# A hybrid decoder layer with mixture of experts: gathers, gain rows and scatter pieces in another order

## The chip, the core and the metric

One core of a Trainium2 chip runs the whole layer as one program. The metric is the device time in microseconds from the first to the last instruction of the core, as the median of three runs. All data are float32. TensorE's matmuls appear in the trace as two records each, one for each pass over a float32 operand, so that "x16" is eight matmuls.

## What is computed

The reference runs one decoder layer over two groups of tokens with shared weights: a prompt of 256 tokens and 8 samples of 8 new tokens each, with 256 cached keys and values behind every sample (D = 1024, 16 heads, 32 experts, 4 chosen for each token). Cut to what matters:

```python
def trunk_layer(x, c, lw, ...):
    ada = silu(c) @ w_ada + b_ada              # shift1, scale1, gate1, shift2, scale2, gate2
    h = rms_norm(x, g_mix_pre) * (1 + sc1) + sh1
    out, st = mixer(h, ...)                    # RG-LRU branch + forgetting attention, @ w_out
    x = x + gt1 * rms_norm(out, g_mix_post)
    h = rms_norm(x, g_ffn_pre) * (1 + sc2) + sh2
    f = moe(h, ...)
    return x + gt2 * rms_norm(f, g_ffn_post)

def expert_block(xb, e):
    gu = xb @ w_gate_up[e] + b_gate_up[e]
    x_glu = minimum(gu[:, :1024], 7.0)
    x_lin = clip(gu[:, 1024:], -7.0, 7.0)
    act = x_glu * sigmoid(1.702 * x_glu) * (x_lin + 1.0)
    return act @ w_down[e] + b_down[e]
```

moe picks the top 4 of 32 experts by softmax of the router's logits and adds up each token's four expert rows with their weights. The outputs are both groups' rows and the new keys, values, log forget values and states.

## The kernel before

Every engine has its own list of instructions, written out by hand and in order; engines meet only at semaphores (`s["name"]`, counted up by the one and waited for by the other). TensorE works in program order, so whatever it waits for holds up all that stands behind it. PSUM is eight banks B[0] to B[7] of 128 x 512 floats.

The stages in order of time: conditioning, input projections and the attention of the prompt (to about 345 us), then a loop over the 8 samples (b = 0 to 7) that carries the prompt's output projection, second norm, router and ranks in its gaps, then the samples' own output projection, norm and router (about 474 to 498 us), the first gather (to 511 us), the loop over 16 pairs of experts (to about 1455 us), and the final norm.

Weights stream through `ring`, twelve units of 1 MB, used as six slots of two units each. SyncE issues the transfers in order, one of 2048 KB for each slot; for each pair eight for gate and up (`gu_slot`, two for each two tiles, one for each expert of the pair) and four for down (`dn_slot`). Before each it waits until the counter `used` says that TensorE has read the slot's former contents: the ones for gate-up tiles 6 and 7 (counted from 0) wait for tile 1 of the same pair, those for down wait for tiles 3 and 5, the next pair's first two wait for tile 7, and the next four for the down tiles 3 and 7.

The loop of pairs treats 64 slots for each of two experts. On TensorE (`pair`, below) a pair is: eight gate-up tiles (k = 0 to 7, eight matmuls each, into B[0] to B[3]), with the former pair's results scattered to the tokens in between (`combine`, behind k = 0, 1, 2, through B[6] and B[7]), the transposes of the weighted selection behind k = 5 and the bias matmuls behind k = 6; then `gather`, which makes four of the eight column groups of inputs for a later pair (three matmuls for each, two over 128 prompt rows and one over 64 sample rows, B[4] and B[5]); then the transposes of the activation, which wait for VectorE (`act_made`); then eight down tiles into B[4] and B[5]. VectorE clips glu and lin once all eight gate-up tiles are done (`used` at 24), multiplies and adds; ScalarE does the sigmoids and copies PSUM to SBUF. Tile k = 0 needs the gathered inputs (`XT_made`). The loop is a hardware loop of four rounds with four pairs unrolled in each (u = 0 to 3).

The first gather makes the inputs of the first two pairs: eight column groups m, each with two prompt matmuls (K = 128) and one sample matmul (K = 64), in the halves of four banks. The prompt's part of the selection `sel` is ready early (`sel_made` 1), the samples' part (`sel_made` 2) only after their router, top 4 and ranks on VectorE. The post-norm gain rows (`G3`, comp = 5) are made by matmuls with an identity column (`gain_of_prompt`) or with rows of the sample table (`gain_of_sample`), and copied by ScalarE. They are used only in the final norm.

Line 1272 is the transposes' helper and line 1736 the matmuls of `both`, which serves gate-up, bias and down tiles. `hT` and `work` in a row tell which buffer holds the gathered inputs (activations are in `work`).

Of the kernel before, what the change touches and what calls it, by code (L numbers as in the profile page):

```python
# [31 lines left out]
def hybrid_layer(nc, x_prompt, x_sample, cache_k, cache_v, cache_logf, state_conv, state_h, page_table,  # L32
# [11 lines left out]
    NT = D // 128  # L44
    SP_, DB, DS = x_prompt.shape[1], x_sample.shape[0], x_sample.shape[1]
    NS = DB * DS
# [14 lines left out]
    NPC = 5  # L61
    EPS, LIMIT, ALPHA, SCALE, LRU_C = 1e-6, 7.0, 1.702, float(HD) ** -0.5, 8.0
# [5 lines left out]
    with ctx:  # L68
# [131 lines left out]
        def piece(v, i):  # L200
            return v[:, 512 * i:512 * i + 512]

        x1 = kf
        G3 = gaf[:, 0:1536]
# [239 lines left out]
        def _(eng):  # L444
# [73 lines left out]
            eng.wait_ge(s["router_ps"], 2)  # L518
# [28 lines left out]
        def _(eng):  # L547
# [107 lines left out]
            for b in range(DB):  # L655
                if b + 2 < DB:
                    keys(b + 2)
                if b + 1 < DB:
                    probs(b + 1)
                if b + 2 < DB:  # L660
                    sexps(b + 2)
                if b == 0:
                    for n, i in enumerate((0, 2, 1, 3)):
                        if n % 2 == 0:
                            eng.wait_ge(s["gain_ps"], n // 2 + 1)
                            A_(piece(G1, n // 2), B[7][:, :], ACT.Copy).then_inc(s["G1_made"], 1)
                        eng.wait_ge(s["op_ps"], n + 1)
                        A_(piece(tokf, i), B[5 + n % 2][:, :], ACT.Square, accum_out=ss[:, i:i + 1]).then_inc(s["op_sq"], 1)
                    root(r1, 2)
                if b == 1:  # L670
                    for i in range(4):
                        eng.wait_ge(s["x1_made"], i + 1)
                        A_(piece(tokf, i), piece(x1, i), ACT.Square, accum_out=ss[:, 4 + i:5 + i]).then_inc(s["x1_sq"], 1)
                    root(r2, 3)
                if b == 3:
                    for k in range(2):
                        for h in range(2):
                            eng.wait_ge(s["h2T_ps"], 2 * k + h + 1)
                            A_(h2P[:, 4 * h:4 * h + 4, 128 * k:128 * k + 128], B[5 + h][:, :].rearrange("p (m n) -> p m n", m=4),
                               ACT.Copy).then_inc(s["h2T_made"], 1)  # L680
                if b == 4:
                    eng.wait_ge(s["topmax_made"], 1)
                    A_(tope[:, 0:2, 0:TOPK], tope[:, 0:2, 0:TOPK], ACT.Exp).then_inc(s["topexp_made"], 1)

# [12 lines left out]
            eng.wait_ge(s["op_ps"], 5)  # L697
            for i in range(3):
                eng.wait_ge(s["G3_ps"], i + 1)
                A_(piece(G3, i), B[3 + i][:, :], ACT.Copy).then_inc(s["G3_made"], 1)  # L700

# [8 lines left out]
            XT_out(0, 0, 1, 0)  # L710
            for i in range(2):
                eng.wait_ge(s["gather_ps"], 3 + i)
                A_(XT[0][:, 4 + 2 * i:6 + 2 * i, :], B[6 - 4 * i][:, :].rearrange("p (t s) -> p t s", t=2), ACT.Copy)\
                    .then_inc(s["XT_made"], 1)

            def pair(t, i, u):
                eng.wait_ge(s["cT_ps"], t + 1)
# [5 lines left out]
                XT_out(1 - u // 2, u % 2, 2 * t + 5, 4)  # L723
# [9 lines left out]

            for i in range(NPC):
                eng.wait_ge(s["scatter_read"], NPC * done + i + 1)
                A_(piece(work[:, 2048:4608], i), piece(gbf, i), ACT.Square, accum_out=ss[:, 10 + i:11 + i]).then_inc(s["f_sq"], 1)
# [3 lines left out]
        def _(eng):  # L740
# [450 lines left out]
            V_.tensor_copy(C[0:E, :], B[4][0:E, 0:T]).then_inc(s["C_made"], 1)  # L1191
# [55 lines left out]
            def combined(t, n):  # L1247
                eng.wait_ge(s["scatter_ps"], NPC * t + n + 1)
                TTo(piece(gbf, n), piece(gbf, n), B[6 + n % 2][:, :], ALU.add).then_inc(s["scatter_read"], 1)  # L1249
# [5 lines left out]
            for n in range(NPC):  # L1255
                eng.wait_ge(s["f_sq"], n + 1)
                link.later(TTo(piece(gbf, n), piece(gbf, n), piece(G3, n if n == 1 else (0, 1, 0, 1, 2)[n]), ALU.mult))
# [10 lines left out]
        def _(eng):  # L1268
# [333 lines left out]
            for b in range(DB):  # L1602
# [24 lines left out]
                if b == 5:  # L1627
                    ranks_of_prompt()
                sfold(b)
            eng.wait_ge(s["wt_made"], 6)  # L1630
# [20 lines left out]
            def gather_first(m, tiles):  # L1651
                out = B[GBANK[m // 2]][:, QUAD * (m % 2):QUAD * (m % 2) + QUAD]
                for k in tiles:
                    q = 64 * (m // 4)
                    if k < 2:
                        last = mm(out, tok[:, k, 128 * m:128 * m + 128], sel[:, k, :], start=(k == 0), stop=False)
                    else:
                        last = mm(out, tok[q:q + 64, 2, 128 * (m % 4):128 * (m % 4) + 128], sel[q:q + 64, 2, :], start=False, stop=True)
                return last
# [4 lines left out]
            for m in (0, 2):  # L1664
                gather_first(m, (0, 1))
            eng.wait_ge(s["x1_sq"], 5)
            both_halves(1)
            eng.wait_ge(s["mo_made"], 5)
            for m in (4, 6):
                gather_first(m, (0, 1))  # L1670
# [3 lines left out]
            last.then_inc(s["h2T_ps"], 1)  # L1674
            eng.wait_ge(s["h2T_made"], 5)
# [7 lines left out]
            for h in range(2):  # L1683
                gain_of_prompt(B[3 + h], 5, h).then_inc(s["G3_ps"], 1)
            gain_of_sample(B[5], 5).then_inc(s["G3_ps"], 1)
# [3 lines left out]
            mm(B[7][:, 224:256], ones[0:64, :], chosen[0:64, 2, :], start=True, stop=True).then_inc(s["rank_ps"], 1)  # L1689
            eng.wait_ge(s["sel_made"], 2)  # L1690
            for m in range(NT):
                last = gather_first(m, (0, 1, 2) if m % 2 else (2,))
                if m % 2:
                    last.then_inc(s["gather_ps"], 1)
# [12 lines left out]
            eng.wait_ge(s["G3_made"], 2)  # L1707
            for k in range(TT):
                last = tr(B[4][0:E, 128 * k:128 * k + TROWS[k]], wtok[0:TROWS[k], k, :], TROWS[k])
# [5 lines left out]
            def combine(t, pieces):  # L1715
                for n in pieces:
# [5 lines left out]
                    k, bank = n // 2, B[6 + n % 2]  # L1722
                    if k < 2:
                        last = mm(bank[:, :], C[:, 128 * k:128 * k + 128], Ysb[:, 512 * (n % 2):512 * (n % 2) + 512], start=True, stop=True)  # L1724
                    else:
                        for h in range(2):
                            last = mm(bank[64 * h:64 * h + 64, :], C[:, SP_:T], Ysb[:, 512 * h:512 * h + 512], start=True, stop=True)
# [11 lines left out]
            def pair(t, i, u):  # L1739
                slots = XT[u // 2][:, :, SL * (u % 2):SL * (u % 2) + SL]  # L1740
                ready = 2 * t + (2 if u % 2 == 0 else 0)
                for k in range(NT):
# [9 lines left out]
                    if k < 3:  # L1752
                        combine(t, ((0, 1), (2, 3), (4,))[k])
                    if k == 5:
# [7 lines left out]
                    if k == 6:  # L1762
# [3 lines left out]
                if u % 2 == 0:  # L1766
                    eng.wait_ge(s["sel_made"], t + 4)
                gather(u % 2, 4)
# [18 lines left out]
            eng.wait_ge(s["f_sq"], NPC)  # L1787
# [34 lines left out]
```

## Time and profile before

| what | value |
|---|---|
| runs, median (lowest to highest) | 1473.31 us (1472.67 to 1474.71) |
| profiled execution, span | 1472.5 us |
| TensorE busy | 1379.4 us, 94% of the span |
| VectorE, ScalarE, GpSimd busy | 340.9, 231.5, 25.5 us |
| mean granted TensorE clock | 0.966 |
| HBM read | 481.63 MB, 330 GB/s over the span |
| chain that ended last | TensorE 76%, DMA 17%, issue 2%, VectorE 2%, ScalarE 2% |
| gate-up transfers in that chain | 16% |

Times are from the start of the span. The profiled execution is one run of its own; its span stands 0.8 us below the median of the timed runs. "Busy" of TensorE counts matmuls whose ends are modelled. A clock of 1.00 is 2.4 GHz and the lower level is 1.2 GHz; a mean between them is a share of time at either. In a timeline row the bracket tells how long the engine was idle before it and what released it.

### The profile page before, as it was taken

What the parts mean: (1) busy time and instruction counts of PE and PEld (TensorE: products, weight loads), DVE (VectorE), ACT (ScalarE), POOL (GpSimd) and SP (SyncE); (2) the same over time, 40 slices, a digit from 0 to 9 for tenths busy, and PEclk for the clock granted to TensorE, in tenths of its full rate; (3) what the DMA queues carried; (4) which work ended last, traced back from release to release, by engine and by line L of the source; (5) the groups of instructions that cost most, each with busy time, mean ns of one, the idle gap of its engine ahead of it and who ended that gap; (6) DMA issues with size and microseconds to landing.
All of it is one profiled execution on the core that took longest, in us unless ns stands there. A gap on an engine that the chain in (4) does not pass through costs nothing.

```text
span 1472.5 us, 15902 instructions
## 1 busy us (share of the span) xinstructions
PE 1379.4 (94%) x6323; PEld 627.4 (43%) x6323; DVE 340.9 (23%) x715; ACT 231.5 (16%) x459; POOL 25.5 (2%) x56
## 2 busy tenths in 40 slices
PE   5999799999988999999999999999999999999996
PEld 3555356666445433434334334333343333433432
DVE  2541412444143320102201111021021010120113
ACT  2113301433251200101111001011010011110102
POOL 1100000001000000000000000000000000000000
PEclk9999899999986899999999999999999999999998
DMA  9836355543056589999999999999999999999992
GB/s 329 258 127 252 111 211 187 189 147 122 15 173 239 214 337 419 428 428 426 429 426 427 428 421 427 430 426 427 426 425 429 426 414 414 422 429 428 428 427 104
DMA packets 72477, 486.84 MB, mean 331 GB/s; under 512 B 10349, under 2 KB 15205, under 8 KB 47828
## 3 DMA queue, kind: packets, MB, share of 16 engines
q1 hardware_dynamic: 70724, 480.85, 80.0%
q0 software_dynamic: 1680, 4.91, 1.0%
q8 instruction: 58, 0.95, 0.3%
q14 instruction: 15, 0.12, 0.0%
HBM read 481.63 MB, written 4.12 MB: 330 GB/s over the span
## 4 chain that ended last, share of the span: by engine, by line
PE 76%; DMA 17%; issue 2%; DVE 2%; ACT 2%; SPq 1%; DVEq 0%; ACTq 0%; PEldq 0%
PE bank L1736 35%; DMA ring<-in_w_gate_up_dram 16%; PE bank L1383 9%; PE bank L1701 5%; PE bank L1410 4%; PE bank L1272 4%; PE bank L1724 3%; PE bank L1702 3%; PE bank L1364 2%; PE bank L1570 2%; PE bank L1527 1%; DMA ring<-in_w_ada_dram 1%; PE bank L1376 1%; PE bank L1363 1%; PE bank L1638 1%
## 5 line engine op out<-in xcount | busy, mean ns | idle before, releaser
L1736 PE MATMUL bank<-ring,work 128*64 128x512 f32 x2048 | 457.6, 600 | 17.7 <-issue 10.3
L1736 PEld LDWEIGHTS bank<-ring,work 128*64 128x64 f32 x2048 | 161.4, 138 | 292.1 <-issue 291.8
L1736 PE MATMUL bank<-ring,hT 128*64 128x512 f32 x1024 | 233.9, 603 | 14.8 <-DMA ring<-in_w_gate_up_dram 14.8
L1249 DVE TENSOR_TENSOR gbT<-gbT,bank 128x512 f32<-128x512 f32 x85 | 58.5, 688 | 452.5 <-PE bank L1724 391.9
L1383 PE MATMUL bank<-hT,ring 128*128 128x320 f32 x512 | 143.4, 440 | 2.4 <-DVE hT L767 1.7
L1736 PEld LDWEIGHTS bank<-ring,hT 128*64 128x64 f32 x1024 | 77.2, 138 | 160.1 <-issue 160.1
L1383 PEld LDWEIGHTS bank<-hT,ring 128*128 128x128 f32 x512 | 97.7, 193 | 50.4 <-issue 8.6
L1218 DVE TENSOR_SCALAR work<-bank 128x512 f32<-128x512 f32 x32 | 22.0, 687 | 323.2 <-PE bank L1736 323.2
L1410 PE MATMUL bank<-hT,ring 128*128 128x320 f32 x256 | 72.4, 436 | 0.0
L1701 PE MATMUL bank<-qT,tok 128*128 128x256 f32 x256 | 72.4, 405 | 0.0
L718 ACT ACTIVATE work<-bank 128x320 f32<-128x320 f32 x16 | 7.0, 437 | 409.9 <-PE bank L1272 409.9
L1724 PE MATMUL bank<-work 128*128 128x512 f32 x136 | 67.4, 618 | 1.2 <-ACT work L730 1.2
L1701 PEld LDWEIGHTS bank<-qT,tok 128*128 128x128 f32 x256 | 43.4, 189 | 32.2 <-issue 28.9
L1410 PEld LDWEIGHTS bank<-hT,ring 128*128 128x128 f32 x256 | 47.4, 190 | 20.1 <-issue 2.3
L730 ACT ACTIVATE work<-bank 128x512 f32<-128x512 f32 x32 | 17.4, 595 | 217.6 <-PE bank L1736 217.6
L1272 PE MATMUL bank<-ident,work 128*128 128x128 f32 (+4 forms) x253 | 44.6, 296 | 6.0 <-DMA work<-in_b_ada_dram 4.0
L1364 PE MATMUL bank<-ring 128*32 128x512 f32 x192 | 29.9, 716 | 19.8 <-DMA ring<-in_w_ada_dram 10.8
L721 ACT ACTIVATE work<-work 128x512 f32<-128x512 f32 x32 | 20.1, 630 | 166.9 <-DVE work L1218 166.9
L1702 PE MATMUL bank<-qT,tok 64*128 64x256 f32 x128 | 44.5, 428 | 0.0
L1272 PEld LDWEIGHTS bank<-ident,work 128*128 128x128 f32 (+4 forms) x253 | 30.5, 175 | 32.6 <-issue 30.1
L1724 PEld LDWEIGHTS bank<-work 128*128 128x128 f32 x136 | 22.9, 189 | 45.1 <-issue 41.8
L1272 PE MATMUL bank<-ident,ring 128*128 128x128 f32 (+2 forms) x139 | 23.9, 329 | 8.1 <-ACT work L637 7.2
(336 smaller groups left out, 882.5 us busy)
## 6 DMA issues: line engine op xcount, KB each, us to landing
ring<-in_w_gate_up_dram SPq DMA_DIRECT2D x128, 2048.0 KB, 14.8
ring<-in_w_down_dram SPq DMA_DIRECT2D x64, 2048.0 KB, 17.0
ring<-in_w_ada_dram SPq DMA_DIRECT2D x12, 2048.0 KB, 9.9
ring<-in_w_in_dram SPq DMA_DIRECT2D x12, 2048.0 KB, 9.9
ring<-in_cache_k_dram SPq DMA_DIRECT2D x16, 512.0 KB, 5.9
ring<-in_cache_v_dram SPq DMA_DIRECT2D x16, 512.0 KB, 4.5
ring<-in_w_out_dram SPq DMA_DIRECT2D x2, 2048.0 KB, 7.7
out_dram<-tok POOLq DMA_DIRECT2D x2, 1024.0 KB, 5.2
```

The lines of the kernel that those rows point to most:

```text
L721: A_(sig[:, 512 * j:512 * j + 512], glu[:, 512 * j:512 * j + 512], ACT.Sigmoid, scale=ALPHA)\
L1218: TS(glu[:, half[j]], B[j][:, :], LIMIT, None, ALU.min).then_inc(s["glu_made"], 1)
L1249: TTo(piece(gbf, n), piece(gbf, n), B[6 + n % 2][:, :], ALU.add).then_inc(s["scatter_read"], 1)
L1272: return nc.tensor.transpose(out, in_, ident[0:rows, 0:rows])
L1364: last = mm(ps[32 * g:32 * g + 32, :], silu_c[:, k, :], w[0][:, k, :], start=(k < 4), stop=(k >= 4))
L1383: last = mm(ps[:, 0:T], w[0][:, k, 128 * (t % 4):128 * (t % 4) + 128], hT[:, k, :], start=(k == 0), stop=(k == NT - 1))
L1410: last = mm(B[4 + h % 2][:, 0:T], w[0][:, k, 128 * (h % 4):128 * (h % 4) + 128], hT[:, k, :], start=(k == 0), stop=(k == NT - 1))
L1570: last = mm(B[5 + t][:, :], gaT[:, k, 128 * t:128 * t + 128], w[h][:, k, :], start=(k == 0), stop=(k == NT - 1))
L1701: mm(out, tok[:, k, 128 * m:128 * m + 128], sel[:, k, :], start=(k == 0), stop=False)
L1702: last = mm(out, tok[q:q + 64, 2, 128 * (m % 4):128 * (m % 4) + 128], sel[q:q + 64, 2, :], start=False, stop=True)
L1724: last = mm(bank[:, :], C[:, 128 * k:128 * k + 128], Ysb[:, 512 * (n % 2):512 * (n % 2) + 512], start=True, stop=True)
L1736: last = mm(bank[CAP * x:CAP * x + CAP, :], lhsT[:, CAP * x:CAP * x + CAP], rhs(x), start=start, stop=stop)
```

## The change

Five edits, in the order of the program.

1. Gain rows of the final norm: they are made in the samples' loop, one each at b = 5, 6, 7, instead of behind the samples' router, and go into the prompt columns of gaT (`G3(i)`, a view of two blocks of 256). ScalarE copies each at the end of its step.
2. First gather: all prompt matmuls of all eight m's stand ahead of the samples' selection, spread over the waits of the samples' norm and router. The two m's of a bank form one accumulation group. The sample matmuls follow in the order 0, 4, 1, 5, 2, 6, 3, 7, so that rows 0 to 63 and 64 to 127 take turns. The transposes of the routing weights go to B[7] instead of B[4], so C is copied in two pieces. The gate-up bias rows' DMAs no longer wait for the samples' router.
3. In a pair, `gather` runs behind the fifth gate-up tile (k = 4) instead of behind the eighth, and the bias matmuls behind k = 5 instead of k = 6. ScalarE copies the gathered rows first in the pair.
4. Scatter pieces run in the order 4, 0, 1, 2, 3 (the sample's first).
5. In the tail, a Sqrt of one element on ScalarE stands ahead of the squares, and the sum of the samples' halves waits for the first square instead of all five.

```diff
+    SCATTER = (4, 0, 1, 2, 3)
-        G3 = gaf[:, 0:1536]
+        def G3(i):
+            return gaT[:, 2 * i:2 * i + 2, 0:SP_]
@@ gpsimd
-            eng.wait_ge(s["router_ps"], 2)
             for j in range(4):
                 eng.dma_start(bgu[E * j:E * j + E, :], ...)
@@ scalar
+                if b >= 5:
+                    eng.wait_ge(s["G3_ps"], b - 4)
+                    A_(G3(b - 5), B[5 + b % 2][:, :].rearrange("p (t n) -> p t n", t=2), ACT.Copy).then_inc(s["G3_made"], 1)
...
-            eng.wait_ge(s["op_ps"], 5)
-            for i in range(3):
-                eng.wait_ge(s["G3_ps"], i + 1)
-                A_(piece(G3, i), B[3 + i][:, :], ACT.Copy).then_inc(s["G3_made"], 1)
...
-            XT_out(0, 0, 1, 0)
-            for i in range(2):
-                eng.wait_ge(s["gather_ps"], 3 + i)
-                A_(XT[0][:, 4 + 2 * i:6 + 2 * i, :], B[6 - 4 * i][:, :].rearrange("p (t s) -> p t s", t=2), ACT.Copy)\
-                    .then_inc(s["XT_made"], 1)
+            for i, (m, bank) in enumerate(((0, 0), (4, 6), (2, 1), (6, 2))):
+                eng.wait_ge(s["gather_ps"], 1 + i)
+                A_(XT[0][:, m:m + 2, :], B[bank][:, :].rearrange("p (t s) -> p t s", t=2), ACT.Copy).then_inc(s["XT_made"], 1)
             def pair(t, i, u):
+                XT_out(1 - u // 2, u % 2, 2 * t + 5, 4)
                 eng.wait_ge(s["cT_ps"], t + 1)
...
-                XT_out(1 - u // 2, u % 2, 2 * t + 5, 4)
                 for j in range(2):
                     eng.wait_ge(s["aT_ps"], 2 * t + (j + 1))
...
-            for i in range(NPC):
-                eng.wait_ge(s["scatter_read"], NPC * done + i + 1)
+            A_(sst[:, 0, 0:1], ones[:, 0:1], ACT.Sqrt)
+            for n, i in enumerate(SCATTER):
+                eng.wait_ge(s["scatter_read"], NPC * done + n + 1)
@@ vector
-            V_.tensor_copy(C[0:E, :], B[4][0:E, 0:T]).then_inc(s["C_made"], 1)
+            link.later(V_.tensor_copy(C[0:E, 0:SP_], B[7][0:E, SP_:2 * SP_]))
+            link(V_.tensor_copy(C[0:E, SP_:T], B[7][0:E, 0:NS]))
+            eng.sem_inc(s["C_made"], 1)
@@ tensor, samples' loop
                 if b == 5:
                     ranks_of_prompt()
+                    gain_of_prompt(B[6], 5, 0).then_inc(s["G3_ps"], 1)
+                if b == 6:
+                    gain_of_prompt(B[5], 5, 1).then_inc(s["G3_ps"], 1)
+                if b == 7:
+                    eng.wait_ge(s["wt_made"], 6)
+                    eng.wait_ge(s["G3_made"], 1)
+                    gain_of_sample(B[6], 5).then_inc(s["G3_ps"], 1)
                 sfold(b)
-            eng.wait_ge(s["wt_made"], 6)
+            eng.wait_ge(s["G3_made"], 3)
             gain_of_sample(B[6], 2).then_inc(s["gains_ps"], 1)
@@ tensor, first gather
+            def gather_prompt(m):
+                for k in range(2):
+                    mm(first_out(m), tok[:, k, 128 * m:128 * m + 128], sel[:, k, :], start=(m % 2 == 0 and k == 0), stop=False)
+            def gather_sample(m):
+                q = 64 * (m // 4)
+                return mm(first_out(m), tok[q:q + 64, 2, 128 * (m % 4):128 * (m % 4) + 128], sel[q:q + 64, 2, :],
+                          start=False, stop=(m % 2 == 1))
             eng.wait_ge(s["sel_made"], 1)
-            for m in (0, 2):
-                gather_first(m, (0, 1))
+            gather_prompt(0)
+            gather_prompt(1)
...
+            eng.wait_ge(s["mo_made"], 5)
+            gather_prompt(4)
             eng.wait_ge(s["h2T_made"], 5)
...
-            for h in range(2):
-                gain_of_prompt(B[3 + h], 5, h).then_inc(s["G3_ps"], 1)
-            gain_of_sample(B[5], 5).then_inc(s["G3_ps"], 1)
+            gather_prompt(5)
+            gather_prompt(6)
             eng.wait_ge(s["chosen_made"], 2)
...
+            gather_prompt(7)
             eng.wait_ge(s["sel_made"], 2)
-            for m in range(NT):
-                last = gather_first(m, (0, 1, 2) if m % 2 else (2,))
-                if m % 2:
-                    last.then_inc(s["gather_ps"], 1)
+            for m in range(4):
+                for q in (m, m + 4):
+                    last = gather_sample(q)
+                    if m % 2:
+                        last.then_inc(s["gather_ps"], 1)
@@ tensor, pair
+                    if k == 4:
+                        if u % 2 == 0:
+                            eng.wait_ge(s["sel_made"], t + 4)
+                        gather(u % 2, 4)
                     if k == 5:
...
-                    if k == 6:
                         eng.wait_ge(s["esel_made"], t + 1)
                         for j in range(4):
                             both(B[j], esel[E * j:E * j + E, :], lambda x: bgu[E * j:E * j + E, :], False, False)
-                if u % 2 == 0:
-                    eng.wait_ge(s["sel_made"], t + 4)
-                gather(u % 2, 4)
                 for j in range(2):
                     eng.wait_ge(s["act_made"], 2 * t + (j + 1))
...
-            eng.wait_ge(s["f_sq"], NPC)
+            eng.wait_ge(s["f_sq"], 1)
```

## Rows read from the trace of the kernel before

**Rows 1.** The page: the span, and the DMA engines' busy tenths in forty slices.
```profile
span 1472.5 us, 15902 instructions
...
DMA  9836355543056589999999999999999999999992
```

**Rows 2.** Stages by pair: busy us and count of PE, PEld, DVE, ACT, POOL; clock, DMA share, GB/s.
```profile
611.00:672.00 61.00, 58.29 (x258) 22.72 (x258) 9.66 (x16) 5.38 (x11) 0.00 (x0) 0.97 1.01 429
672.00:729.00 57.00, 56.24 (x255) 21.70 (x255) 9.43 (x15) 4.89 (x10) 0.00 (x0) 1.00 1.00 427
```

**Rows 3.** The chain in order of time, where a pair's down tiles begin.
```profile
554.56 17.39 PE bank L1736 x80
...
611.26 17.39 PE bank L1736 x80
...
1440.97 13.97 PE bank L1736 x64
```

**Rows 4.** TensorE's waits from 511 to 1456 us: total, times, longest.
```profile
PE bank L1736 <- DMA ring<-in_w_gate_up_dram: 21.5, 13, 2.1
```

**Rows 5.** The chain inside one pair: the transfer that the seventh gate-up tile waits for.
```profile
1108.08 18.67 DMA ring<-in_w_gate_up_dram
```

**Rows 6.** Timeline of the same pair, from the end of the eighth gate-up tile on.
```profile
1135.10 1.13 PE L1701 MATMUL bank<-qT,tok 128*128 128x256 f32 x4
...
1138.22 0.68 DVE L1231 TENSOR_TENSOR work<-work 128x512 f32<-128x512 f32 x1
...
1139.54 0.69 DVE L1231 TENSOR_TENSOR work<-work 128x512 f32<-128x512 f32 x1
...
1141.85 1.23 PE L1272 MATMUL bank<-ident,work 128*128 128x128 f32 x8
...
1143.32 3.22 PE L1736 MATMUL bank<-ring,work 128*64 128x512 f32 x14 [0.25 <-issue]
```

**Rows 7.** Timelines of TensorE around idle gaps, in the samples' loop and the pairs.
```profile
410.97 1.10 PE L1272 MATMUL bank<-ident,ring 128*128 128x128 f32 x8 [0.23 <-DMA ring<-in_cache_k_dram]
416.30 1.97 PE L1272 MATMUL bank<-ident,ring 128*128 128x128 f32 x8 [4.24 <-ACT work L637]
...
949.16 3.65 PE L1736 MATMUL bank<-ring,hT 128*64 128x512 f32 x16 [2.12 <-DMA ring<-in_w_gate_up_dram]
981.51 5.35 PE L1736 MATMUL bank<-ring,work 128*64 128x512 f32 x16 [1.96 <-issue]
```

**Rows 8.** Timeline of the first gather, from the gain rows to the first gate-up tile.
```profile
494.01 1.13 PE L1550 MATMUL bank<-xT,ident 32*128 32x512 f32 x4
...
497.43 0.42 DVE L1122 TENSOR_TENSOR qT<-xT,qT 128x256 f32<-128x256 f32 x1
...
499.06 2.07 PE L1656 MATMUL bank<-qT,tok 128*128 128x256 f32 x4
...
509.18 1.13 PE L1656 MATMUL bank<-qT,tok 128*128 128x256 f32 x4
510.24 0.70 PE L1658 MATMUL bank<-qT,tok 64*128 64x256 f32 x2
...
511.81 3.65 PE L1736 MATMUL bank<-ring,work 128*64 128x512 f32 x16 [0.39 <-ACT work L713]
```

**Rows 9.** Timeline of the samples' loop: one gain row alone, then steps six and seven.
```profile
371.15 1.12 PE L1550 MATMUL bank<-xT,ident 32*128 32x512 f32 x2
...
464.38 1.93 PE L1527 MATMUL bank<-ring,work 128*32 128x256 f32 x16 [3.13 <-DVE gbT L1018]
...
467.95 0.99 PE L1534 MATMUL bank<-work 128*128 128x32 f32 x4
...
472.83 1.06 PE L1534 MATMUL bank<-work 128*128 128x32 f32 x4 [0.55 <-DVE work L1010]
```

**Rows 10.** Timeline of the tail.
```profile
1461.65 3.09 DVE L1257 TENSOR_TENSOR gbT<-gbT,gaT 128x512 f32<-128x512 f32 x5
...
1462.51 1.28 ACT L553 ACT_TABLE_LOAD   x1
```

More of the change, by code:

```diff
@@ L1248, in combined @@
                 eng.wait_ge(s["scatter_ps"], NPC * t + n + 1)
-                TTo(piece(gbf, n), piece(gbf, n), B[6 + n % 2][:, :], ALU.add).then_inc(s["scatter_read"], 1)
+                i = SCATTER[n]
+                TTo(piece(gbf, i), piece(gbf, i), B[6 + n % 2][:, :], ALU.add).then_inc(s["scatter_read"], 1)
             done = moe_rounds(eng, pair)
@@ L1254, in _ @@
             eng.wait_ge(s["G3_made"], 3)
-            for n in range(NPC):
+            for n, i in enumerate(SCATTER):
                 eng.wait_ge(s["f_sq"], n + 1)
-                link.later(TTo(piece(gbf, n), piece(gbf, n), piece(G3, n if n == 1 else (0, 1, 0, 1, 2)[n]), ALU.mult))
+                v = piece(gbf, i).rearrange("p (t n) -> p t n", t=2)
+                link.later(TTo(v, v, G3(2 if i == 4 else i % 2), ALU.mult))
             halves(r3[:, 0:2], ss[:, 10:14])
@@ L1649, in _, with first_out @@
             GBANK = (0, 1, 6, 2)
[L1651 to L1659, printed above, removed]
+            def first_out(m):
+                return B[GBANK[m // 2]][:, QUAD * (m % 2):QUAD * (m % 2) + QUAD]
+            def gather_prompt(m):
[5 more added lines that the diff above has]
+                          start=False, stop=(m % 2 == 1))
             eng.wait_ge(s["op_sq"], 5)
@@ L1663, in _ @@
             eng.wait_ge(s["sel_made"], 1)
-            for m in (0, 2):
-                gather_first(m, (0, 1))
+            gather_prompt(0)
+            gather_prompt(1)
             eng.wait_ge(s["x1_sq"], 5)
             both_halves(1)
-            eng.wait_ge(s["mo_made"], 5)
-            for m in (4, 6):
-                gather_first(m, (0, 1))
+            gather_prompt(2)
+            gather_prompt(3)
             eng.wait_ge(s["h2tok_made"], 5)
@@ L1706, in _ @@
             eng.wait_ge(s["wtok_made"], 2)
-            eng.wait_ge(s["G3_made"], 2)
             for k in range(TT):
-                last = tr(B[4][0:E, 128 * k:128 * k + TROWS[k]], wtok[0:TROWS[k], k, :], TROWS[k])
+                o = SP_ + 128 * k if k < 2 else 0
+                last = tr(B[7][0:E, o:o + TROWS[k]], wtok[0:TROWS[k], k, :], TROWS[k])
             last.then_inc(s["wt_ps"], 1)
@@ L1721, in combine @@
                         eng.wait_ge(s["scatter_read"], NPC * t + (n - 1))
-                    k, bank = n // 2, B[6 + n % 2]
+                    i, bank = SCATTER[n], B[6 + n % 2]
+                    k = i // 2
                     if k < 2:
-                        last = mm(bank[:, :], C[:, 128 * k:128 * k + 128], Ysb[:, 512 * (n % 2):512 * (n % 2) + 512], start=True, stop=True)
+                        last = mm(bank[:, :], C[:, 128 * k:128 * k + 128], Ysb[:, 512 * (i % 2):512 * (i % 2) + 512], start=True, stop=True)
                     else:
```

## The prediction

> **What bounds the kernel now.** I read the page's slices first: over the loop of pairs TensorE is busy nearly all the time (94% of the whole span) and, from slice 14 on, the DMA engines are at nine tenths or more [rows 1]. Two things are that full at once, so the question is which of them ends last, and by how much. The stages by pair of experts answer it [rows 2]: DMA share 1.00 and some 427 GB/s in every pair, TensorE busy 58.29 of 61 us in one and 56.24 of 57 in the next. A pair brings twelve transfers of 2048 KB (2.097 MB); at 427 GB/s one takes 4.91 us and twelve take 58.9. The first down tile of pair 0 starts at 554.56 and that of pair 15 at 1440.97 [rows 3]: 886.4 us for 15 periods, 59.1 each. So the mean pair is the DMA's. How far behind is TensorE? The pair from 554.56 to 611.26 has no wait for a transfer: 56.7 us. That is TensorE's own need, and the whole slack is 59.1 - 56.7 = 2.4 us. The waits confirm it: 21.5 us for gate-up weights in 13 waits, over 16 pairs [rows 4]. In the chain a pair therefore alternates between TensorE and the wait for the seventh gate-up tile's weights [rows 5].
>
> **The move of a pair's gathers.** Before, the eight gathers stand between the eighth gate-up tile and the activation's transposes. The timeline of a pair [rows 6] shows what they do there. TensorE ends that tile at 1135.10. VectorE and ScalarE then need the clips, sigmoids and products: the first half of the activation is ready at 1138.22 + 0.68 = 1138.90, the second at 1139.54 + 0.69 = 1140.23. The gathers run from 1135.10 to 1141.85, 6.7 us, and hide all of it; transposes and 0.25 of issue bring the down tiles to 1143.32, 8.2 us after the tile's end. After the change the gathers run behind the fifth gate-up tile and still take 6.7. But nothing is left to cover the activation. Transposes of half 0 can start 3.8 us after the eighth tile; those of half 1 wait until 5.1, take 0.6 (half of 1.23), and with 0.25 of issue the down tiles start 6.1 us after the tile's end. ScalarE's copies of half 0 are done by then, because the gathered rows' copies have moved out of its way. So a pair costs TensorE 6.7 + 6.1 - 8.2 = 4.6 us more: about 61.3 instead of 56.7. That is more than the DMA's 58.9, and the bound changes hands.
>
> Does the DMA queue keep up? SyncE issues two slots' transfers whenever their counter is passed. The transfers for tiles seven and eight are issued after the second tile and wanted at the seventh, some 25 us later with the gathers now in between. They took 18.7 us with a full queue [rows 5]; with over 2 us of slack in each period the queue drains, so less. The next pair's first two are issued after the eighth tile, which comes about 4.6 us later within the pair, and are wanted only after a whole down stage of 13.8 us plus 6.1. TensorE waits for none of them. What goes in return: the 21.5 us of waits, and what they cost in clock. The fetch stalls of some 2 us at the loop's branch (three in all, one stands at 981.51 [rows 7]) stay.
>
> **The clock.** After idle gaps of about 2.1 us the granted clock sometimes fell to the lower level, 1.2 GHz: the tile behind the gap took 5.35 us instead of 3.65, 1.70 more, at 981.51, but not at 949.16 [rows 7]. Five of the loop's sixteen stages show 0.97 for this reason (one of them in rows 2); three of the falls stood behind DMA waits (3 x 1.7 = 5.1 us, returned with them). The new gap is 3.8 us, then 0.6 of transposes, then 0.7 of idle. No gap of the loop is that long. The nearest outside it is 4.24 us before 416.30: eight transposes then took 1.97 instead of 1.10 [rows 7], 0.9 more, with the low clock reaching on into the work behind them. So I expect a fall in most pairs, costing 0.9 to 1.7 us each; I take 1.5, nearer the rows inside the loop. Bounds: 0 (as at 949.16) and 2.5 (a longer low stretch, as from 499 to 506, where groups of gathers took 2.07 instead of 1.13 [rows 8]). The Trainium skill (TensorE: Matmul & The Clock Gate, section HAM oscillation) says that idle phases between bursts let the clock fall again and again, each time at a price. By that rule the fall comes in all 16 pairs, and the sum below stands as it is.
>
> **First gather.** Before, select of the sample ends at 497.43 + 0.42 = 497.85 and the first pair starts at 511.81, 14.0 us: gathers until 510.87, part at the low clock, then ScalarE's last copy, which releases the first tile [rows 8]. After, all sixteen prompt matmuls have run ahead: four of the m's as before, one in the wait for the copy of h2T, two in place of the post-norm rows from 494.01 on, one while VectorE ranks. Behind select stand eight sample matmuls, 0.53 each at 256 columns and the high clock (four records of line 1656 in 1.06, as at 509.18). Do two row halves overlap? Two post-norm rows from different row quarters (the four records at 494.01) took 1.13 together, as one alone does (two records at 371.15, 1.12; the next group starts 1.05 later in both cases) [rows 8, 9]; so four steps of 0.53, 2.1 us, then two of ScalarE's copies, about 0.6 each, and hand-over, about 4.0 in all. The Trainium skill (TensorEngine Tiling, section Key Properties) says that row tiles load and multiply in parallel and that a change of tiling mode drains the array. By it the halves take 2.1 us too. Without overlap they take 8 x 0.63 = 5.0 (0.63 is what two records of line 1658 advance). Gain 14.0 - 4.0 = 10.0; 0.4 is lost because one m's prompt gathers (1.05) are longer than the wait of about 0.7 that they fill.
>
> **Post-norm rows in the samples' loop.** One such row costs 1.05 at the high clock, so about 2.0 at the low one. The first is hidden: TensorE idles 3.13 us before 464.38. The second sits between the transposes and the fold at 467.95, for which VectorE and then the next values wait: 1.05 to 2.0, all on the path. The third stands before the fold at 472.83, behind 0.55 of idle: 0.5 to 1.45 [rows 9]. Sum 1.6 to 3.5; the stretch is mostly at the low clock, so I take 2.5. ScalarE's copies (0.60) hide behind the fold (0.99). Net start of the loop: 10.0 - 0.4 - 2.5 = 7.1 us earlier; bounds 3 (no overlap, low clock) and 9.
>
> **The rest, at nothing.** The tail's early Sqrt saves a table load of 1.28 at 1462.51 that ends at 1463.79, while VectorE multiplies until 1464.74 [rows 10]: hidden already; uncovered it would be worth 1.3. The order of pieces and the earlier sum move at most 0.1. The gate-up bias rows come earlier on GpSimd's queue; nothing of the loop's start waits for them before, where ScalarE's last copy released it [rows 8]. The two chained copies of C (one small instruction more, some 0.3) end before the first combine; if they did not, that 0.3 would count once.
>
> **Sum against the profiled 1472.5.** 16 x (4.6 + 1.5) = +97.6; waits and their clock back -(21.5 + 5.1) = -26.6; start -7.1. Together +63.9: 1536.4, and with the 0.8 by which the median of the runs (1473.3) stands above the profiled span, 1537.
>
> **Rivals.** (A) The clock holds in every gap: 16 x 4.6 - 26.6 - 7.1 = +40, 1513. For it: 949.16; against: that gap is half as long as the new one. (B) Other side, faster: the loop stays with the DMA, because the uncovered activation wait fits the slack, so that only the start's 7.1 is left, 1466. It decides by one number: it holds if the added TensorE time is under 2.2 us (58.9 - 56.7), and the rows give 4.6. (C) The low clock lasts some 7 us each time, 3.4 per pair: 16 x 8.0 - 33.7 = +94, 1568. For it: the stretch from 499 to 506; against: every fall inside the loop cost 1.7. (D) The halves don't overlap, so that part of the change doesn't do what it says: +2.9 on the forecast, 1540, inside the range.
>
> **How the numbers follow.** Forecast with D 0.68, A 0.15, C 0.08, B 0.07, 0.02 for a wash of gains and losses. Range: from no clock loss with the largest start gain, +73.6 - 26.6 - 9 = +38 (1511), to 2.5 per pair with the smallest, +113.6 - 26.6 - 3 = +84 (1557); rounded outward for the 0.2 us by which a reading per pair can be off, 1508 to 1560. It leaves out B and C. A measurement of this kernel can tell about 0.2%, 3 us, from no change. Faster 0.07, same 0.02, slower 0.91.
>
> **What would show it.** Periods between first down tiles of 61 to 64 us, all alike but for the branch; DMA share about 0.94 and some 400 GB/s; no wait for gate-up weights; a TensorE gap of 3.8 us behind each eighth tile ended by VectorE; first down tiles slowed, PEclk 0.96 to 0.97 in each pair; first pair near 504.7. I am wrong if the periods stay at 59, if the gap is below 2.2 us, or if TensorE still waits for weights.

## The result, and the profile after

The changed kernel takes 1537.3 us in the median (1533.8 to 1547.3), the kernel before 1473.2: 1.044 times as long, with a 95% interval of 1.041 to 1.048. The forecast was 1537.

The profiled execution of the changed kernel is its slowest, 1545.3 us. Three lines of its page, beside [rows 1]: the DMA engines are no longer full in every slice of the loop, and the chain has given up the transfers (1% instead of 17%) for TensorE and VectorE.

```profile
span 1545.3 us, 15904 instructions
...
DMA  8636365433247689999999999998999999999991
...
PE 88%; DVE 5%; issue 3%; ACT 2%; DMA 1%; SPq 0%; DVEq 0%; ACTq 0%; PEldq 0%
```

The same stages as in [rows 2], one pair each; the columns are the stretch, its length, the busy time of PE, PEld, DVE, ACT and POOL, the granted clock, DMA share and GB/s. Both clock and DMA share are now below 1.00 in every pair.

```profile
1068.90:1132.10 63.20, 58.99 (x258) 20.86 (x259) 9.49 (x15) 5.17 (x9) 0.00 (x0) 0.96 0.96 399
1132.10:1196.10 64.00, 59.64 (x257) 21.02 (x259) 9.44 (x16) 5.17 (x9) 0.00 (x0) 0.95 0.94 394
```

TensorE's waits inside the loop, which answer [rows 4]. The wait for gate-up weights is gone. In its place stand 32 waits for line 1233, VectorE's last product of each activation half, 66.4 us in all, or 4.15 a pair. Line 1276 is the transposes' helper here, and line 1752 the matmuls of `both`.

```profile
PE bank L1276 <- DVE work L1233: 66.4, 32, 3.8
PE bank L1752 <- issue: 6.3, 3, 2.2
```

The timeline of one pair from the end of its eighth gate-up tile on, which answers [rows 6]. The profile models that end at 1125.84; the prediction counted from the start of the next instruction, which overlaps it by 0.06, so that 1125.78 is the point to compare with 1135.10.

```profile
1125.89 0.69 DVE L1220 TENSOR_SCALAR work<-bank 128x512 f32<-128x512 f32 x1 [25.30 <-PE bank L1752]
...
1129.63 0.90 PE L1276 MATMUL bank<-ident,work 128*128 128x128 f32 x4 [3.79 <-DVE work L1233]
...
1130.95 1.13 PE L1276 MATMUL bank<-ident,work 128*128 128x128 f32 x4 [0.43 <-DVE work L1233]
...
1132.01 16.35 PE L1752 MATMUL bank<-ring,work 128*64 128x512 f32 x64
```

TensorE stands still for 3.79 us, transposes half 0, waits 0.43 for half 1 and starts the down tiles 6.2 us behind the eighth tile. The transposes take 0.90 and 1.13 instead of the 0.6 that is half of 1.23 in [rows 6], the down tiles 16.35 instead of 13.97 [rows 3]. The granted clock (before the DMA share) shows why:

```profile
1125.90:1130.00 4.10, 0.37 (x3) 0.38 (x4) 4.10 (x7) 1.26 (x2) 0.00 (x0) 1.00 0.99 424
1130.10:1136.80 6.70, 6.27 (x19) 2.29 (x19) 2.73 (x5) 1.20 (x2) 0.00 (x0) 0.50 1.00 428
```

It has fallen to the lower level behind the gap and stays there into the down tiles.

The first gather, beside [rows 8] and [rows 9]. First the gain rows at b = 6 and b = 7, then the select, the eight sample matmuls and the first gate-up tile.

```profile
475.79 2.07 PE L1554 MATMUL bank<-xT,ident 32*128 32x512 f32 x2
...
482.13 1.97 PE L1559 MATMUL bank<-xT 32*64 32x512 f32 x4
...
508.55 0.42 DVE L1122 TENSOR_TENSOR qT<-xT,qT 128x256 f32<-128x256 f32 x1
...
509.03 2.00 PE L1671 MATMUL bank<-qT,tok 64*128 64x256 f32 x16
...
512.50 3.65 PE L1752 MATMUL bank<-ring,work 128*64 128x512 f32 x16 [0.77 <-ACT work L713]
```

The whole difference between the two profiled spans, 72.8 us (1545.3 - 1472.5), by stretches:

| stretch | before | after | difference |
|---|---|---|---|
| start to a fixed point in the samples' loop (values, b = 4) | 440.27 | 447.98 | +7.7 |
| from there to the first gate-up tile | 71.5 | 64.5 | -7.0 |
| pair 0, to its first down tile | 42.8 | 47.9 | +5.1 |
| 15 periods between first down tiles | 886.4 (59.1 each) | 951.6 (63.4 each) | +65.2 |
| from the last pair's down tiles to the end | 31.5 | 33.4 | +1.8 |

The first row is no effect of the change. It arises before any changed instruction, by 40 us, and begins with the 48 records that turn x. The lines below are the changed kernel's, then the kernel before's:

```profile
19.14 14.18 PE L1297 MATMUL bank<-gbT,tok 128*128 128x128 f32 x48 [0.17 <-PE bank L1368]
...
19.05 8.45 PE L1293 MATMUL bank<-gbT,tok 128*128 128x128 f32 x48 [0.17 <-PE bank L1364]
```

The cause is when TensorE's clock first rises. The trace of the changed kernel has its first record of a granted clock, a rise to the full level, at 37.8 us; that of the kernel before has it at 19.8. The stretches of the profile count the time ahead of the first record as full, but the matmuls show that it was the lower level. In the changed kernel one form of matmul, 512 columns at line 1368, takes (its columns: shortest, median and longest in ns):

```profile
L1368 PE MATMUL bank<-ring x12: 1061/1061/1062, 35.1 to 36.8; 128*32 128x512 f32 x12
...
L1368 PE MATMUL bank<-ring x36: 592/592/657, 37.7 to 43.9; 128*32 128x512 f32 x36
...
L1368 PE MATMUL bank<-ring x32: 1033/1061/1062, 179.4 to 190.0; 128*32 128x512 f32 x32
```

The third line lies in a stretch that the profile itself gives as 0.50 (178 to 194 us). The profiled runs fall into two groups. In three (changed, e2, e5) the first rise stands at 37.6 to 38.1 us, and they are 7.4 to 8.1 us behind the kernel before at 40 us; in the other nine it stands at 17.7 to 19.8, and they are at most 1.2 us away from it. Why the rise comes late in some executions of the same work stays open.

A second chance of the same kind lies in the samples' loop. e1 and e10 below are one kernel (run on two chips; e1's own twelve runs lie between 1457.5 and 1472.4), yet their first gate-up tiles start at 498.46 and 504.61. The difference grows from 350 us on, where the low stretches that begin before 455 us add up to 13.7 us in e1 and 27.3 in e10. The two profiles of the result don't differ there: the changed one is 7.7 to 7.9 us behind all the way from 40 to 440 us. So the total of a single run carries a chance of 7 to 8 us at the start and of about 6 us in the samples' loop, and I read the loop of pairs by its periods and the start by intervals between fixed points.

### The profile page after: what moved, and what is told of

Its sections match the earlier page's. It is cut to its first block, busy times and chain, and to the rows that moved or that the text cites. A ratio compares the mean times of both kernels' runs of the same rounds, so it can differ in the third digit from the quotient of the medians.

```text
span 1545.3 us, 15904 instructions
## 1 busy us (share of the span) xinstructions
PE 1414.6 (92%) x6323; PEld 612.3 (40%) x6323; DVE 340.0 (22%) x716; ACT 233.4 (15%) x460; POOL 25.5 (2%) x56
## 4 chain that ended last, share of the span: by engine, by line
PE 88%; DVE 5%; issue 3%; ACT 2%; DMA 1%; SPq 0%; DVEq 0%; ACTq 0%; PEldq 0%
PE bank L1752 46%; PE bank L1387 9%; PE bank L1716 4%; PE bank L1740 4%; PE bank L1414 4%; PE bank L1276 4%; PE bank L1717 3%; PE bank L1574 2%; PE bank L1368 2%; DVE work L1228 1%; PE bank L1531 1%; PE bank L1743 1%; PE bank L1297 1%; DVE work L1233 1%; DMA ring<-in_w_ada_dram 1%
## 5 line engine op out<-in xcount | busy, mean ns | idle before, releaser
L1752 PE MATMUL bank<-ring,work 128*64 128x512 f32 x2048 | 475.3, 619 | 7.0 <-issue 6.3
L1752 PEld LDWEIGHTS bank<-ring,work 128*64 128x64 f32 x2048 | 146.7, 143 | 318.2 <-issue 318.2
L1752 PE MATMUL bank<-ring,hT 128*64 128x512 f32 x1024 | 229.9, 596 | 0.0
L1752 PEld LDWEIGHTS bank<-ring,hT 128*64 128x64 f32 x1024 | 69.7, 137 | 150.9 <-issue 150.9
L1276 PE MATMUL bank<-ident,work 128*128 128x128 f32 (+4 forms) x253 | 58.9, 355 | 72.4 <-DVE work L1233 66.4
L1276 PEld LDWEIGHTS bank<-ident,work 128*128 128x128 f32 (+4 forms) x253 | 36.0, 180 | 113.1 <-DVE work L1233 85.6
L1740 PE MATMUL bank<-work 128*128 128x512 f32 x136 | 71.6, 631 | 0.0
L729 ACT ACTIVATE work<-bank 128x512 f32<-128x512 f32 x32 | 17.4, 595 | 235.4 <-PE bank L1752 235.4
L708 ACT ACTIVATE hT<-bank 128x512 f32<-128x512 f32 x16 | 9.6, 597 | 223.8 <-PE bank L1717 223.8
L708 ACT ACTIVATE work<-bank 128x512 f32<-128x512 f32 x16 | 9.6, 598 | 220.4 <-PE bank L1717 220.4
L1740 PEld LDWEIGHTS bank<-work 128*128 128x128 f32 x136 | 21.5, 188 | 49.3 <-issue 47.4
```

The lines of the kernel that those rows point to most:

```text
L1276: return nc.tensor.transpose(out, in_, ident[0:rows, 0:rows])
L1752: last = mm(bank[CAP * x:CAP * x + CAP, :], lhsT[:, CAP * x:CAP * x + CAP], rhs(x), start=start, stop=stop)
```

## The experiments

From each trace I take the start of the first gate-up tile, the mean period (first down tile of pair 0 to that of pair 15, over 15) and what lies between that first tile and the end, which the chances ahead of it don't touch. The totals are medians of the timed runs, the ratios are against the kernel before on the same chip.

| kernel | total, us | ratio (95%) | mean period | first tile to end |
|---|---|---|---|---|
| before | 1473.2 | | 59.1 | 960.7 |
| changed | 1537.3 | 1.044 (1.041 to 1.048) | 63.4 | 1032.8 |
| e1 gathers back | 1462.8 | 0.993 (0.991 to 0.996) | 59.0 | 958.7 |
| e2 move alone | 1549.7 | 1.051 (1.045 to 1.056) | 63.4 | 1032.1 |
| e3 two late | 1467.1 | 0.997 (0.993 to 1.000) | 58.9 | 959.6 |
| e4 one late | 1504.4 | 1.022 (1.017 to 1.026) | 61.7 | 1005.0 |
| e5 filled gap | 1513.4 | 1.027 (1.023 to 1.030) | 61.9 | 1008.0 |
| e6 before, half down | 1447.6 | 0.983 (0.980 to 0.987) | 57.4 | 935.8 |
| e7 changed, half down | 1539.0 | 1.045 (1.041 to 1.049) | 63.6 | 1035.5 |

**e1: the move undone.** All other edits stay. ScalarE's copies of the gathered rows go back behind the sigmoids with it.

```diff
-                    if k == 4:
-                        ...
-                        gather(u % 2, 4)
...
+                gather(u % 2, 4)
                 for j in range(2):
                     eng.wait_ge(s["act_made"], 2 * t + (j + 1))
```

> The changed kernel with one thing undone: a pair's gathers stand behind the eighth gate-up tile again (and ScalarE's copies of them behind the sigmoids); all other edits stay. Theory (the move uncovered the activation wait and made TensorE the bound): the whole loss is gone and only the start's gain of 7 us is left, 1466 us, periods of 59.1 us, DMA share 1.00 in each pair. Rival (the loss comes from the other edits in or before the loop, or from the order of the pieces): it stays well above 1473.

Measured 1462.8, 0.66% (0.36 to 0.95%) below the kernel before, with periods of 59.0 and the DMA share back at 1.00. So the loss hangs on the move. The 10.3 us below the kernel before are more than the start's 7: from the first tile to the end the profile of e1 takes 2.0 us less than before, and the medians carry the chances named above. The waits for weights are back too, as more and on average shorter ones (13 waits in 21.5 us before [rows 4]):

```profile
PE bank L1752 <- DMA ring<-in_w_gate_up_dram: 22.4, 29, 2.4
```

**e2: the move alone**, in the kernel before: the same lines of `pair` moved on TensorE and on ScalarE, nothing at the start or in the tail.

> The kernel before with the move alone: gathers behind the fifth gate-up tile, the bias matmuls behind the sixth, ScalarE's copies first. Theory: 16 uncovered waits, +72 us as the profile of the changed kernel shows them (5.2 in pair 0, 65.2 over 15 periods, 1.7 behind the last), so 1545 us. Rival (the edits act together): not the sum of the two parts, below 1530 or above 1555.

From the first tile to the end it takes 71.4 us more than before, against 72.1 in the changed kernel. The total of 1549.7 is 77 above before; its four runs scatter from 1538 to 1555, and the profiled one carries the 14.18 at the start. Up to that scatter the parts add up: e2 is 76.6 and e1 -10.3 us from the kernel before, together 66.3, and the changed kernel 64.1. Nothing shows the edits acting on each other.

**e3 and e4: how much cover is enough.** Two column groups (e3) or one (e4) of four stay behind the eighth tile. In both, ScalarE copies the first two groups' rows first in the pair and the other two behind the sigmoids; these lines are left out here.

```diff
-                        gather(u % 2, 4)
+                        gather(u % 2, 4, range(0, 2))      # e4: range(0, 3)
...
+                gather(u % 2, 4, range(2, 4))              # e4: range(3, 4)
                 for j in range(2):
                     eng.wait_ge(s["act_made"], 2 * t + (j + 1))
```

> The changed kernel with the gathers split: two column groups behind the fifth tile, two (3.4 us) behind the eighth. Theory: the down tiles still start 6.1 us after the eighth tile, so TensorE needs 56.7 + 3.4 + 6.1 - 8.2 = 58.0 us a pair, under the transfers' 58.9: nothing is lost, 1466 to 1469 us. Rival (moving gathers ahead of the sixth to eighth tiles frees the ring's slots later and starves the DMA queue, in proportion to what is moved): half of the loss, about 1500 us.

> As the former, but three column groups behind the fifth tile and one (1.7 us) behind the eighth. Theory: TensorE needs 56.7 + 5.0 + 6.1 - 8.2 = 59.6 us a pair, just over the transfers' 58.9, and has a gap of 2.1 us in each, behind which the clock falls about every second time (0.8): with the branch's stalls some 60.5 to 60.9, so 1490 to 1498 us; 1478 if the clock holds. Rival (loss in proportion to what is moved): three quarters of it, 1520 us.

e3 has the loop of e1 (959.6 against 958.7 us) though half of the gathers moved. Its TensorE has gaps of 0.42 and 0.58 us in each pair, which the transfers' slack pays. The clock falls behind them in one pair of 16 (at 1188.4). A pair without wait or branch takes 57.8 us:

```profile
1012.00:1069.80 57.80, 56.80 (x257) 20.36 (x257) 9.18 (x14) 5.17 (x9) 0.00 (x0) 1.00 1.01 428
...
1067.77 0.75 PE L1277 MATMUL bank<-ident,work 128*128 128x128 f32 x4 [0.42 <-DVE work L1234]
1069.09 0.74 PE L1277 MATMUL bank<-ident,work 128*128 128x128 f32 x4 [0.58 <-DVE work L1234]
```

So the loss is not in proportion to what is moved, and earlier gathers don't starve the DMA queue. It begins between e3 and e4, where TensorE's need (57.8 us in e3, 59.6 by the working for e4) passes the transfers' 58.9. e4 is past that point, as expected, but with 61.7 rather than 60.5 to 60.9. The gap has the size I worked out, and what I mis-sized is how often the clock falls behind it:

```profile
1036.40 1.12 PE L1277 MATMUL bank<-ident,work 128*128 128x128 f32 x4 [2.10 <-DVE work L1234]
1037.72 1.13 PE L1277 MATMUL bank<-ident,work 128*128 128x128 f32 x4 [0.20 <-DVE work L1234]
```

A gap of 2.0 to 2.3 us in the loop before was followed by a fall in 5 of 11 cases [rows 7]. In e4 the trace has a fall in each of the 16 pairs. Here a second gap of 0.2 to 0.6 follows after one short burst; that this second gap makes the difference is likely but not tested. In the thirteen pairs whose down tiles the branch doesn't interrupt, they take 0.5 to 2.0 us longer than in e5, where the clock holds.

**e5: the gap filled.** Seven matmuls more in each pair, into a bank that nobody reads at that point.

```diff
+                for _ in range(7):
+                    mm(B[6][:, 0:256], tok[:, 0, 0:128], tok[:, 1, 0:256], start=True, stop=True)
                 for j in range(2):
                     eng.wait_ge(s["act_made"], 2 * t + (j + 1))
```

> The changed kernel with seven matmuls more in each pair, behind the eighth gate-up tile, into a bank that nobody reads (seven times 0.53 us = 3.7): they fill the wait for the activation and move nothing else. Theory (part of the loss is the clock, which falls in the gap): the clock stays at 1.00, the periods fall from 63.4 to 61.4 us and the time to about 1510 us. Rival (the wait alone is the loss, the clock costs nothing): 1537 us as before, or more if the fillers delay the transposes.

TensorE does more work and the kernel is 24 us faster than the changed one. Of the gaps only 0.57 and 0.58 us are left. The clock holds at 1.00 but for two falls behind the branch's stall (16 falls in the changed kernel), and a pair without the branch takes 61.2 us:

```profile
1056.70:1117.90 61.20, 60.05 (x272) 22.94 (x271) 9.19 (x14) 5.17 (x9) 0.00 (x0) 1.00 0.98 410
...
862.92 3.29 PE L1786 MATMUL bank<-tok 128*128 128x256 f32 x14
866.78 0.75 PE L1276 MATMUL bank<-ident,work 128*128 128x128 f32 x4 [0.57 <-DVE work L1233]
868.10 0.74 PE L1276 MATMUL bank<-ident,work 128*128 128x128 f32 x4 [0.58 <-DVE work L1233]
868.78 3.65 PE L1752 MATMUL bank<-ring,work 128*64 128x512 f32 x16
```

The mean period falls from 63.4 to 61.9: the clock costs 1.5 us a pair, the uncovered wait the other 2.8 above the 59.1 before.

**e6 and e7: fewer bytes.** Half of each down transfer is left out in both kernels, so half of each down slot holds older data and the expert outputs are not the layer's.

```diff
-                    eng.dma_start(dn_slot[g], dnv[g // 2, :, ds(2 * i + g % 2, 1), :, :]...)
+                    eng.dma_start(dn_slot[g][:, 0:2, :], dnv[g // 2, :, ds(2 * i + g % 2, 1), 0:2, :]...)
```

> The kernel before with half of each down transfer left out (the other half of the slot keeps older data), so that a pair brings ten transfers' worth of bytes instead of twelve: 49 us. Theory (the transfers bound it by 2.4 us a pair): waits for weights vanish, periods of 57.0 us, 1473 - 27 = 1446 us. Rival (TensorE bounds it already): 1473 us.

> The changed kernel with the same half of each down transfer left out. Theory (TensorE bounds it): no change, 1537 us within its scatter of some 5 us, periods of 63.4. Rival (the transfers still bound it, because the slots come free later): 20 us or more are gained.

Before: 25 us faster; a pair takes 56.9 us with the DMA engines 0.89 busy. Changed: nothing (1539.0 against 1537.3; 1.045 and 1.044 of the kernel before), with the DMA engines 0.82 busy. Each of the two was run twice.

```profile
1012.50:1069.40 56.90, 56.30 (x255) 21.81 (x256) 9.53 (x15) 5.09 (x10) 0.00 (x0) 1.00 0.89 369
```

```profile
933.50:995.70 62.20, 58.21 (x258) 20.86 (x259) 9.49 (x15) 5.17 (x9) 0.00 (x0) 0.97 0.82 338
```

This shows the exchange of bounds by itself: the transfers bound the kernel before and do not bound the changed one.

**e8: row halves in turn.** The kernel of e1 with the sample matmuls in the order 0 to 7.

> The kernel of e1 with the eight sample matmuls of the first gather in the order 0 to 7, so that rows 0 to 63 and 64 to 127 no longer take turns. Theory (two row halves run at once): 8 x 0.53 to 0.63 instead of 2.0 us for the eight, the loop starts 2.3 to 3 us later than in e1, 1469 us. Rival (the order makes no difference): 1466 us, as e1.

Measured 1462.8, as e1; the totals can't tell 3 us. The trace can. The eight matmuls in e8:

```profile
494.09 2.96 PE L1671 MATMUL bank<-qT,tok 64*128 64x256 f32 x16
```

2.96 us against 2.00 in e1, so the alternation saves 1.0 us and not 3. But the order 0 to 7 does not keep the halves apart, as I had meant it to. Line 1671 in three stretches, with the busy time and count of records of PE and PEld; the first two are e8's, the third e1's:

```profile
494.09:495.05 0.96, 0.96 (x4) 0.85 (x5) 1.00 0.87 358
495.06:495.80 0.74, 0.74 (x8) 0.73 (x7) 1.00 0.11 44
...
494.99:495.95 0.96, 0.96 (x8) 0.88 (x10) 1.00 0.68 273
```

In e8 one half works alone for 0.97 us, a record every 0.216; then the other half starts beside it and the records come twice as fast. In e1 both halves start together. The signals say the same: in e8 the records that report m = 3, 5 and 7 done start 1.62, 1.73 and 2.59 us behind the first record, so m = 5 of the second half ends just behind m = 3 of the first. In either order the four matmuls of one half take 1.99 us from first start to last end. One after the other the two halves would take 4.0 us by this, an estimate; in the changed order they take 2.00, and in e8 2.96 because half of the overlap is left. So the halves overlap fully, and e8 shows half of what that is worth.

On the way from select to the first tile only 0.4 of the 1.0 is left (3.91 us against 3.53). ScalarE's first copy starts 1.2 us behind the first sample matmul in both, and in e8 only the second one waits once more, 0.27 us. The prediction's size for no overlap was wrong as well: it took 0.63 for a K = 64 matmul from a sequence that mixes K = 64 and K = 128; within one half they take 0.43.

**e9: gain rows in the tail.** The kernel of e1 with the three rows out of the samples' loop, made behind the pairs; e10 is e1 beside it.

```diff
+            for h in range(2):
+                gain_of_prompt(B[h], 5, h).then_inc(s["G3_ps"], 1)
             combine(done, range(NPC))
+            gain_of_sample(B[2], 5).then_inc(s["G3_ps"], 1)
```

> The kernel of e1 with the three post-norm rows taken out of the samples' loop altogether: they are made behind the loop of pairs, the prompt's two in the 1.2 us in which TensorE waits for the last down tiles' copies, the sample's behind the last pieces, and VectorE multiplies straight from their banks. Theory (the rows cost 3.4 us on the samples' path, as the profile of the changed kernel shows: 2.0 at b = 6, 1.4 at b = 7): the first pair starts 3.4 us earlier, the tail grows by 0.4 (five products at 0.69 instead of 0.62), 3 us less than e1 on the same chip. Rival (that path has slack and the rows were hidden): as e1, or 0.4 slower.

> The kernel of e1 beside e9, to compare the two on one chip: both theories expect e1's time again, 0.5 to 0.7% below the kernel before.

1459.7 for both, 0.991 and 0.992 of the kernel before, with intervals of 0.3% to either side: inconclusive on 3 us. In the traces, from the values of b = 6 to VectorE's merge, e9 takes 471.40 - 461.59 = 9.8 us and e10 477.47 - 464.17 = 13.3. So the rows do cost 3.5 us there. The tail grows by 0.5 (from the last pair's down tiles to the end 32.0 against 31.5), and from the first tile to the end e9 takes 959.7 against 958.7. That the whole is about 3 us faster is likely by this, but not shown by the totals.

Both e1 and e9 beat the kernel before by 0.7 to 0.9%, clear of their intervals.

## Why the prediction was right, step by step

**The bound before.** Right: 59.1 a pair by the transfers, 56.7 by TensorE. With fewer bytes (e6) a pair without the branch takes 56.9. The branch's stalls, which I called fetch stalls, stand in the profile only as "issue"; what they are stays open.

**The uncovered wait.** Right in mechanism and nearly in size: 6.1 us expected from the eighth tile to the down tiles, 6.2 seen, with gaps of 3.79 and 0.43. The terms as written (5.1 + 0.6 + 0.25) add up to 6.0, a slip of 0.1 a pair or 1.6 us in all. With the clock held, e5 has 5.9 from tile to tile (862.92 to 868.78), and a pair of 61.2 against my 61.3. So about 0.4 of the 6.2 belongs to the clock, which slows the second half's transposes. That TensorE would wait for no transfer held too; e3 and e7 rule out the starved queue.

**The clock.** 1.5 us a pair was taken and 1.5 is what e5 gives back (63.4 - 61.9). That a fall comes in every pair was guessed from a single longer gap. It does: the granted clock is 0.94 to 0.98 in pair 0 and in each of the 15 periods, and the trace has 16 falls in the 16 pairs, where the loop before has 5. That the size hit exactly is luck within the 0 to 2.5 that I allowed: the down tiles lengthen by anything from 0.5 to 2.4 us. So rival A (the clock holds, 1513) is what e5 measured, 1513.4, when the gap is filled; from the first tile to the end e5 takes 47.3 us more than before, and A's terms for that stretch give 73.6 - 26.6 = 47.0. Rival C (a low stretch of 7 us in each pair at 3.4 us) had the length partly right and the price wrong. The low stretches of the changed loop add up to 81.9 us, 5.1 a pair and up to 6.8. They begin 2.4 to 5.1 us behind the eighth tile, so that a part of each falls into the wait, where a slow TensorE costs little. Rival B fails at its own threshold: 4.6 us against a slack of 2.2; e3, whose uncovered part is under the slack, is where B's result of "only the start is left" appears.

**The sum.** For everything from pair 0 on I had +97.6 - 26.6 = +71.0; the profiles differ by 72.1. The start gave -7.0 against -7.1, but in other portions, so that this agreement is luck: the gain rows cost 3.5 in the samples' loop rather than 2.5 (13.3 against 9.8 us from the values of b = 6 to the merge; 2.0 and 1.45 were my upper bounds, and the clock is low there), the 0.4 for the longer gather did not appear, and from select to the first tile it is 3.5 us rather than 4.0. Rival D (no overlap of the row halves) is refuted: they overlap fully, 2.00 us as the forecast had it (2.1). Its price of 2.9 us was too high too, since without overlap the matmuls would take 4.0 us and not 5.0.

**The tail.** Right as far as it can be seen: from the last pair's down tiles to the end 31.5 in e1 and before, so the early Sqrt's table load is worth nothing there.

**What the forecast didn't have.** The chances of 7 to 8 us at the start and of 6 us in the samples' loop. The agreement of the total within 1 us is therefore luck, closer than the method is. What the method gave is the loop, 71.0 us against 72.1, and single terms of the start that were off by up to 1 us each.

## What to carry to other kernels

Before moving work forward on an in-order engine, ask what it hides where it stands. Count the dependent chain behind it to its end (here 5.1 us of VectorE and ScalarE) and compare what becomes uncovered with the slack of the loop's real bound: below the slack a move costs nothing (e3), above it each microsecond is paid in every round. Such a gap on TensorE can cost more than its length: filling the 3.8 us here with useless matmuls was faster than leaving them empty, and leaving the useful ones there was better still.

## What the runs showed of the hardware

- Two gaps with a short burst between them (2.1 us, transposes, then 0.2 to 0.6) were followed by a fall of the granted clock in 16 of 16 pairs of e4, and so were the gap of 3.79 us and the one behind it in 16 of 16 pairs of the changed kernel. Single gaps of 2.0 to 2.3 us in the loop before were in 5 of 11 cases, and the two gaps of 0.42 and 0.58 us of e3 in 1 of 16.
- TensorE starts a run at the lower level, and its first rise came at 17.7 to 19.8 us in nine profiled runs and at 37.6 to 38.1 in three, which cost those 7.4 to 8.1 us. The turning of x, 48 records of 128 columns, takes 14.18 us ahead of the rise (421 ns a record) and 8.1 to 8.7 where the rise falls just ahead of it or into its beginning (275 ns a record at the full level). The profile gives 1.00 for the time ahead of the first record of the clock, so there the matmuls' durations are the better witness.
- The four matmuls of K = 64 and 256 columns in one row half take 1.99 us, at one pace (a record every 0.216) whether the other half works beside them or not. Eight take 2.00 us when the halves alternate; one after the other would be 4.0, an estimate from twice 1.99. The Trainium skill (TensorEngine Tiling, section Theoretical Speedup) gives up to 2 for two row tiles, and the trace agrees.
- A matmul leaves two records in these traces and a transpose one (x4 for the four transposes of an activation half). Only that count is used here; that each record of a matmul is one pass over an operand is not shown by any run.
